# The delta rule's inverse: one evacuation moved from VectorE to ScalarE, with a new table of places

## The chip, the cores and the metric

The kernel runs on one core of one Trainium2 chip. The metric is the device time of one execution in microseconds (us). A core has TensorE (PE, and PEld for its weight loads), VectorE (DVE), ScalarE (ACT), GpSimd (POOL) and SyncE (SP), each with its own queue worked off in order; they wait for one another on semaphores. Matmuls write to PSUM banks, from which VectorE and ScalarE copy.

## The reference

Two blocks run one after the other on 1024 tokens of width 1024. The second is a hybrid mixer with a gated delta rule, followed by a mixture of experts. Only the delta rule matters here. Each of 8 heads (keys and values of width 128) runs it twice, over the sequence and over the reversed sequence. In chunks of tokens, with `t_mat` the inverse of a unit triangular matrix:

```
t_mat = inverse(eye + a_mat)          # a_mat strictly triangular, one per chunk
u = t_mat @ (v * beta);  w = t_mat @ (k_beta * exp(g))
def step(state, inp):                 # one chunk after the other
    v_new = u_c - w_c @ state
    o_c = q_c @ state + qk_c @ v_new
    state = state * dec_c + k_c^T @ v_new
```

The outputs of both directions are added, normalized and gated.

## The kernel before, in words

The stage is `delta_scan`. 1040 tokens are 10 chunks of 104 rows. For each head four programs are written once for every engine:

- `prepare(h)`: transposes of v and k (`v 0..2`, `k 0..2`), gaps of decays (`gap`, L2726, 20 instructions of VectorE), their exp (L2857), products k·k and q·k (`kk`, `qk`, L2537), GpSimd's `nbeta` and `strict` (L2946, L2950), transposes `T 0..4` (L2546, copied by ScalarE at L2863). Transposes and products share one PSUM bank, so each waits until the one before is copied out.
- `invert(h)`: the inverses of both directions from 64 by 64 blocks: five rounds over three units of chunks (4, 3 and 3), so 15 pairs (round, unit). In each, TensorE squares the power (`NT`; ScalarE copies both directions out, L2884, in the last round L2886), and multiplies the sum so far (`P`). In the straight direction VectorE adds the bank to `pc` (L2755). In the crossed one GpSimd first adds one to the power (`nti`, L2979), TensorE's product is then the whole new sum, and VectorE only copies it from its bank to `pc` (L2757). The next P waits for both. After the last: `pt`, `ym`, `w`, which put the blocks together.
- `recur(h)`: ten steps k; TensorE makes KS (L2656), VectorE the right-hand side (L2803), TensorE U (L2670), ScalarE copies U (L2904), TensorE dS (L2676) and the outputs (L2682, L2684), VectorE the new state S (L2813) and sums of outputs (L2784, L2793).
- `finish(h)`: squares and VectorE's `ms` (L2825), GpSimd's power and scaling of the outputs (pow L2997, onorm L2999), transposes `y 0..2` (L2702).

While `recur(h)` runs, `invert(h + 1)`, `finish(h - 1)` and `prepare(h + 2)` are spread over its 30 places, three per step: for TensorE, place 3k stands between KS and U, 3k+1 between U and dS, 3k+2 behind the outputs. For VectorE places 3k and 3k+1 stand between the outputs of step k-1 and S, 3k+2 behind S; for ScalarE 3k stands ahead of U's copy. GpSimd has no step of its own, so places give it only an order. The places of every item on every engine are tables (`a_place`, `b_place`, `take_place`, ...). An item is issued in its place or, where an earlier item of its own program has a later one, right behind that item:

```
def upto(self, place):
    while self.place is not None and self.place <= place:
        self.place = next(self.program, None)
```

Two prologues run ahead of head 0: `prepare(0)`, then `invert(0)` with `prepare(1)`. The last two heads have no `prepare` beside them.

Of the kernel before, what the change touches and what calls it, by code (L numbers as in the profile page):

```python
# [19 lines left out]
ACT = mybir.ActivationFunctionType  # L20
# [3 lines left out]
P = 128  # L24
# [2226 lines left out]
def delta_scan(nc, p2T, qT_d, kT_d, vT_d, gc_d, etot_d, sc_d, dmask_d, strict_d, ident_d, eye_d, gout_d, ydT):  # L2251
# [11 lines left out]
    ROUNDS = 5  # L2263
# [3 lines left out]
    with ExitStack() as ctx:  # L2267
# [76 lines left out]
        a_place = {('v', 0): 2, ('v', 1): 3, ('v', 2): 2, ('k', 0): 4, ('k', 1): 6, ('k', 2): 7, ('kk', 0): 11, ('qk', 0): 12, ('kk', 1): 13, ('qk', 1): 14, ('kk', 2): 15, ('qk', 2): 17, ('T', 0): 18, ('T', 1): 16, ('T', 2): 21, ('T', 3): 24, ('T', 4): 27, ('gap', 0, 0, 0): 1, ('gap', 0, 0, 1): 0, ('gap', 1, 0, 0): 0, ('gap', 1, 0, 1): 0, ('gap', 0, 1, 0): 1, ('gap', 0, 1, 1): 3, ('gap', 1, 1, 0): 1, ('gap', 1, 1, 1): 0}  # L2344
        d_place = {('y', 0): 8, ('y', 1): 9, ('y', 2): 10}
        copy_place = {('exp', 0, 0): 3, ('v', 0): 2, ('exp', 1, 0): 0, ('v', 1): 3, ('exp', 0, 1): 1, ('v', 2): 0, ('exp', 1, 1): 0, ('k', 0): 4, ('k', 1): 6, ('k', 2): 7, ('T', 0): 16, ('T', 1): 18, ('T', 2): 23, ('T', 3): 26, ('T', 4): 27}
        fill_place = {('kk', 0): 11, ('qk', 0): 12, ('kk', 1): 13, ('qk', 1): 14, ('kk', 2): 15, ('qk', 2): 17}
# [1353 lines left out]
```

## Time and profile before

| | |
|---|---|
| time, median of 3 runs | 3744.97 us (3739.28 to 3747.4) |
| the profiled execution | 3753.08 us |
| its span, first to last instruction | 3751.3 us |
| mean granted clock of TensorE | 0.938 of full speed |
| the delta stage from its first inverse on | 589.4 us of the span |

The profile is one execution. In timelines each row is one instruction or a run of like ones (start, duration, engine, line, what it writes and reads, count), and in brackets how long the engine was idle before it and who ended that. Busy times of a stretch are followed by the count of instructions. The count of TensorE's fp32 matmuls is two records each.

### The profile page before, as it was taken

To read this page: it belongs to the slowest core of one execution; us is meant where nothing else is said; L and a number is where in the kernel's file an instruction comes from. 1 tells how busy PE (TensorE), PEld (TensorE's weight loads), DVE (VectorE), ACT (ScalarE), POOL (GpSimd) and SP (SyncE) were. 2 spreads that over 40 slices of the span, in tenths; PEclk is the share of its full clock that TensorE was granted. 3 is DMA by queue.
4 is the path that set the end of the run, shared out by engine and by line. 5 is a ranking of instruction groups with operands and counts; after the bars stand their busy time and mean duration, and the time that the engine had idled before them with its cause. 6 is when DMAs were issued, how large, how long until landed. Compare 5 with 4: busy or idle time off the path is not lost. (4 is left out here: it accounts for less than half of the span.)

```text
span 3751.3 us, 80899 instructions
## 1 busy us (share of the span) xinstructions
PE 3210.4 (86%) x33564; PEld 2675.7 (71%) x33564; DVE 1609.8 (43%) x2654; ACT 944.7 (25%) x1831; POOL 572.1 (15%) x615
## 2 busy tenths in 40 slices
PE   8999999888897979999999568888969995988873
PEld 6878777788775768999999457777859773544431
DVE  3155654334335633111989436665544424111113
ACT  2022311122132212100554234444421110211111
POOL 1000000000001000000323044445410001222222
PEclk9999999999998998999999679999979997999997
DMA  4335455321136333332554321111035238999997
GB/s 126 93 119 195 165 202 190 101 54 45 57 129 229 108 105 96 94 96 93 176 173 145 102 79 46 53 53 42 26 110 167 73 88 341 418 419 417 413 412 296
DMA packets 314850, 595.26 MB, mean 159 GB/s; under 512 B 56993, under 2 KB 221706, under 8 KB 285590
## 3 DMA queue, kind: packets, MB, share of 16 engines
q1 hardware_dynamic: 263348, 455.68, 34.3%
q10 hardware_dynamic: 40329, 118.90, 9.0%
q0 software_dynamic: 10928, 17.08, 1.3%
q8 instruction: 196, 3.21, 0.4%
q14 instruction: 49, 0.40, 0.0%
HBM read 472.36 MB, written 139.97 MB: 163 GB/s over the span
## 5 line engine op out<-in xcount | busy, mean ns | idle before, releaser
L3304 PE MATMUL ex_bank_ps<-ex_w_gate_up_sb,ex_xT_sb 128*64 128x256 f32 x2240 | 282.9, 407 | 87.9 <-DMA ex_w_gate_up_sb<-in_w_up_e 82.1
L3304 PEld LDWEIGHTS ex_bank_ps<-ex_w_gate_up_sb,ex_xT_sb 128*64 128x64 f32 x2240 | 166.0, 141 | 216.9 <-issue 125.7
L260 DVE CAST in_w_hi_sb<-in_w_sb 128x1024 fp32r<-128x1024 f32 x119 | 81.9, 688 | 549.4 <-PE in2n_bank_ps L272 268.1
L272 PE MATMUL in2n_bank_ps<-in_h_hi_sb,in_w_hi_sb 128*128 128x352 f32 (+3 forms) x696 | 224.8, 323 | 2.1 <-DVE in_h_lo_sb L401 2.1
L272 PE MATMUL in2n_bank_ps<-in_h_lo_sb,in_w_hi_sb 128*128 128x352 f32 (+3 forms) x696 | 224.2, 322 | 0.0
L272 PE MATMUL in2n_bank_ps<-in_h_hi_sb,in_w_lo_sb 128*128 128x352 f32 (+3 forms) x696 | 223.7, 321 | 0.0
L1474 PE MATMUL mix_bank_ps<-mix_y_hi_sb,mix_wb_hi_sb 128*128 128x512 f32 (+2 forms) x480 | 170.7, 356 | 56.5 <-DVE mix_y_lo_sb L1705 44.8
L3495 DVE TENSOR_TENSOR ex_hidden_sb<-ex_silu_g_sb,ex_bank_ps 128x128 f32<-128x128 f32 x70 | 20.1, 287 | 443.7 <-ACT ex_silu_g_sb L3356 443.7
L1635 POOL TENSOR_TENSOR mix_y_lo_sb<-mix_raw_sb,mix_y_hi_sb 128x1024 fp32r<-128x1024 f32 (+1 forms) x8 | 20.0, 2498 | 1152.1 <-ACT mix_y_hi_sb L1561 1152.1
L272 PE MATMUL qkv_tile_bank_ps<-in_h_hi_sb,in_w_hi_sb 128*128 128x352 f32 (+1 forms) x576 | 186.0, 323 | 8.8 <-DVE qkv_ones_r_sb L1867 7.9
L272 PE MATMUL qkv_tile_bank_ps<-in_h_lo_sb,in_w_hi_sb 128*128 128x352 f32 (+1 forms) x576 | 185.4, 322 | 0.0
L272 PE MATMUL qkv_tile_bank_ps<-in_h_hi_sb,in_w_lo_sb 128*128 128x352 f32 (+1 forms) x576 | 185.2, 322 | 0.0
L1883 DVE SCALAR_TENSOR_TENSOR qkv_y_sb<-qkv_x_sb,qkv_taps_sb,qkv_y_sb 128x1040 f32<-128x1040 f32 x96 | 182.5, 1901 | 3.4
L1474 PE MATMUL mix_bank_ps<-mix_y_lo_sb,mix_wb_hi_sb 128*128 128x512 f32 (+2 forms) x480 | 169.4, 353 | 0.0
L1474 PE MATMUL mix_bank_ps<-mix_y_hi_sb,mix_wb_lo_sb 128*128 128x512 f32 (+2 forms) x480 | 169.2, 352 | 0.0
L272 PE MATMUL prep_tile_bank_ps<-in_h_hi_sb,in_w_hi_sb 128*128 128x512 f32 x384 | 154.5, 402 | 5.1 <-PEq L159 5.1
L272 PE MATMUL prep_tile_bank_ps<-in_h_lo_sb,in_w_hi_sb 128*128 128x512 f32 x384 | 150.8, 393 | 0.0
L272 PE MATMUL prep_tile_bank_ps<-in_h_hi_sb,in_w_lo_sb 128*128 128x512 f32 x384 | 150.6, 392 | 0.0
L262 DVE TENSOR_TENSOR in_w_lo_sb<-in_w_sb,in_w_hi_sb 128x1024 fp32r<-128x1024 f32 x119 | 145.0, 1219 | 4.1
L1474 PEld LDWEIGHTS mix_bank_ps<-mix_y_hi_sb,mix_wb_hi_sb 128*128 128x128 f32 x480 | 92.0, 192 | 68.0 <-issue 55.6
L272 PEld LDWEIGHTS in2n_bank_ps<-in_h_hi_sb,in_w_hi_sb 128*128 128x128 f32 (+1 forms) x696 | 129.4, 186 | 3.9 <-DVE in_h_lo_sb L401 2.5
L272 PEld LDWEIGHTS in2n_bank_ps<-in_h_hi_sb,in_w_lo_sb 128*128 128x128 f32 (+1 forms) x696 | 129.1, 185 | 1.5
(480 smaller groups left out, 8166.7 us busy)
## 6 DMA issues: line engine op xcount, KB each, us to landing
ex_w_gate_up_sb<-in_w_gate_e SPq DMA_DIRECT2D x70, 1024.0 KB, 19.9
ex_w_gate_up_sb<-in_w_up_e SPq DMA_DIRECT2D x70, 1024.0 KB, 29.8
ex_w_down_sb<-in_w_down_e SPq DMA_DIRECT2D x70, 1024.0 KB, 29.6
in_w_sb<-in_w_in SPq DMA_DIRECT2D x118, 512.0 KB
scr_pT<-in_o_sb ACTq DMA_DIRECT2D x65, 512.0 KB
scr_p2T<-in_o_sb ACTq DMA_DIRECT2D x52, 520.0 KB
qkv_x_sb<-scr_p2T SPq DMA_DIRECT2D x8, 1560.0 KB, 8.1
mix_gate_sb<-scr_pT SPq DMA_DIRECT2D x24, 512.0 KB, 3.5
```

The source lines that it names most:

```text
L260: dve.tensor_copy(self.w_hi[:, s, :, 0:width], w).then_inc(self.w_hi_rdy, 1)
L262: dve.tensor_tensor(self.w_lo[:, s, :, 0:width], w, self.w_hi[:, s, :, 0:width].bitcast(F32), ALU.subtract).then_inc(self.w_split, 1)
L272: last = pe.matmul(self.psum(s, n)[:width, 0:m], w_[:, s, k, 0:width], h_[:, k, a:a + m], start=(k == 0 and z == 0), stop=(k == KT - 1 and ...
L1474: last = pe.matmul(bank[:, 4 * s + c, 0:w], w_[:, s, k, :], y_[:, k0[n] + k, a:a + w], start=(k == 0 and z == 0), stop=(k == kts[n] - 1 an ...
L1635: pool.tensor_tensor(y_lo[:, j, :], raw[:, j % RAW, :], y_hi[:, j, :].bitcast(F32), ALU.subtract).then_inc(y_split_pool, 1)
L1883: ins = v.scalar_tensor_tensor(y[:, q, k % 2, :], x[:, u, q, k:k + N], taps[:, u, q, k:k + 1], y[:, q, (k - 1) % 2, :], ALU.mult, ALU.add)
L3304: last = t.matmul(bank[m * BT:(m + 1) * BT, GU_B + b % 2, 0:2 * P], xT[:, s, k, at:at + BT], wgu[:, ws, :, k, m::M], start=(k == 0), stop= ...
L3495: v.tensor_tensor(h[:, s, :], sg[:, s, :], bank[:, GU_B + s, P:2 * P], ALU.mult).then_inc(h_rdy, 1)
```

## The change

ScalarE copies the crossed sums instead of VectorE: same source, same target, same 15 a head. On ScalarE the copy of P(i-1) stands behind the copies of NT(i). Whoever waited for it on VectorE's semaphore (`vx`) waits on ScalarE's (`ax`). All tables of places are new as well.

```diff
-        ax = Plan(st.sem("act_crossed"), [("NT", *w) for w in powers])
+        ax = Plan(st.sem("act_crossed"), [x for x in pe_order if x[0] in ("NT", "P")])
...
-        vx = Plan(st.sem("dve_crossed"), [("pc", z) for z in range(2)] + [("P", *w) for w in powers])
+        vx = Plan(st.sem("dve_crossed"), [("pc", z) for z in range(2)])
...
                         vb.wait(t, h, "P", *powers[i - 1])
-                        vx.wait(t, h, "P", *powers[i - 1])
+                        ax.wait(t, h, "P", *powers[i - 1])
...
                     vb.step(v.tensor_tensor(pc[:, us(u), :], pc[:, us(u), :], blocks(P_B[0], k), ALU.add), "P", r, u)
-                    px.wait(v, h, "P", r, u)
-                    vx.step(v.tensor_copy(pc[:, us(u, 1), :], blocks(P_B[1], k)), "P", r, u)
...
+                def take_sums(r, u):
+                    yield take_place["P", r, u]
+                    px.wait(a_, h, "P", r, u)
+                    ax.step(a_.activation(pc[:, us(u, 1), :], blocks(P_B[1], len(unit(u))), ACT.Copy), "P", r, u)
+
+                for i, w in enumerate(powers):
+                    yield from take_powers(*w)
+                    if i:
+                        yield from take_sums(*powers[i - 1])
+                yield from take_sums(*powers[-1])
```

What the tables come to on TensorE, by place (P r,u and NT r,u: round and unit):

| place | before | after |
|---|---|---|
| 1 | NT 1,0 | NT 1,0 |
| 2 | NT 1,1, v 0 | NT 1,1, P 1,0 |
| 3 | P 1,0, NT 1,2, v 1, v 2 | v 0 |
| 4 | P 1,1, k 0 | NT 1,2, P 1,1, v 1, v 2, k 0 |
| 6 | NT 2,0, k 1 | NT 2,0, k 1 |
| 7 | k 2 | P 1,2, NT 2,1, k 2 |
| 8 | P 1,2, NT 2,1, P 2,0, y 0 | y 0 |
| 9 | NT 2,2, P 2,1, y 1 | P 2,0, NT 2,2, y 1 |
| 10 | NT 3,0, P 2,2, y 2 | P 2,1, NT 3,0, P 2,2, y 2 |
| 14 | P 3,1, qk 1 | qk 1 |
| 15 | NT 4,0, kk 2 | P 3,1, NT 4,0, kk 2 |
| 16 | P 3,2, NT 4,1, P 4,0 | P 3,2, NT 4,1, P 4,0, qk 2 |
| 17 | qk 2 | NT 4,2 |
| 18 | NT 4,2, T 0, T 1 | T 0, T 1 |
| 19 | P 4,1, NT 5,0 | P 4,1, NT 5,0, T 2 |
| 20 | P 4,2 | - |
| 21 | NT 5,1, P 5,0, T 2 | P 4,2, NT 5,1, P 5,0, T 3 |
| 22 | NT 5,2, P 5,1 | NT 5,2 |
| 23 | P 5,2 | P 5,1 |
| 24 | T 3 | P 5,2, T 4 |
| 27 | ym 1, w 0, T 4 | ym 1 |
| 28 | w 1 | w 0, w 1 |

Places 0, 5, 11 to 13, 25, 26 and 29 are the same in both. On the other engines:

- VectorE: of the 20 gap instructions, 13 stood in place 1 and 7 in place 3; now 8 stand in place 1 and 12 in place 3. The sum of P 1,0 goes from place 4 to 2, that of P 5,2 from 23 to 24, the `w` products from 27 to 28.
- ScalarE: `v 0` to `v 2` stay in place 3, ahead of U's copy of step 1. k 2's copy goes from place 7, behind NT 2,1, to place 6, ahead of U's copy of step 2. T 0's copy stays in place 16, and NT 4,2's goes from ahead of it to behind it.
- GpSimd: the order up to `nti 1,2` is nti 1,0, nti 1,1, pow, onorm, nbeta, strict, nbeta, and a second strict that stood ahead of nti 1,2 and now stands behind nti 2,0. `kd` and `strict` change places with `nti 3,0`.

## Rows read from the trace of the kernel before

**Rows 1.** The page of the kernel before: span, busy time and share by engine
```profile
span 3751.3 us, 80899 instructions
...
PE 3210.4 (86%) x33564; PEld 2675.7 (71%) x33564; DVE 1609.8 (43%) x2654; ACT 944.7 (25%) x1831; POOL 572.1 (15%) x615
```

**Rows 2.** Stretches of the delta stage
```profile
core 0: us, PE busy (x) PEld busy (x) DVE busy (x) ACT busy (x) POOL busy (x), PEclk, DMA share, GB/s
2193.40:2250.80 57.40, 45.36 (x1573) 39.35 (x1576) 26.66 (x74) 24.60 (x55) 32.37 (x35) 0.94 0.11 29
...
2461.60:2531.50 69.90, 62.74 (x1638) 55.98 (x1631) 43.16 (x131) 30.69 (x90) 33.73 (x36) 0.98 0.19 55
...
sum 589.40, PE 505.60 PEld 447.86 DVE 337.13 ACT 240.56 POOL 262.01; mean PE 56.18 PEld 49.76 DVE 37.46 ACT 26.73 POOL 29.11
```

**Rows 3.** TensorE's waits, heads 1 to 5: total us, times, longest
```profile
PE dlt_bank_ps L2557 <- DVE dlt_o_sb L2793: 8.0, 5, 1.7
...
PE dlt_bank_ps L2546 <- ACT dlt_qkT_sb L2863: 4.3, 5, 0.9
PE dlt_bank_ps L2702 <- ACT dlt_ktok_sb L2850: 3.6, 5, 0.8
...
PE dlt_bank_ps L2670 <- DVE dlt_rh_sb L2803: 1.7, 5, 0.3
```

**Rows 4.** VectorE's groups by form, the stage: busy us, mean ns
```profile
L2757 DVE COPY dlt_p_blocks_sb<-dlt_bank_ps 128x192 f32<-128x192 f32 x80 | 28.0, 350 | 0.0
...
L2757 DVE COPY dlt_p_blocks_sb<-dlt_bank_ps 128x256 f32<-128x256 f32 x40 | 16.7, 417 | 0.0
```

**Rows 5.** ScalarE's groups by form, the stage
```profile
L2886 ACT ACTIVATE dlt_powers_sb<-dlt_bank_ps 128x192 f32<-128x192 f32 x32 | 8.7, 325 | 19.9 <-PE dlt_bank_ps L2557 19.9
```

**Rows 6.** Timeline of TensorE: first inverse, then fourth head
```profile
2202.97 0.27 PE L2557 MATMUL dlt_bank_ps<-dlt_p_blocks_sb,dlt_powers_sb 64*64 64x64 f32 x2 [0.93 <-ACT dlt_powers_sb L2884]
...
2471.25 0.43 PE L2525 MATMUL dlt_bank_ps<-dlt_ident_sb,dlt_vT_sb 128*104 128x128 f32 x2 [0.69 <-ACT dlt_vtok_sb L2850]
...
2473.21 0.61 PE L2676 MATMUL dlt_bank_ps<-dlt_U_sb,dlt_k_decayed_sb 104*128 104x128 f32 x4
...
2476.71 0.49 PE L2670 MATMUL dlt_bank_ps<-dlt_rh_sb,dlt_p_sb 104*104 104x128 f32 x3
...
2477.95 0.42 PE L2525 MATMUL dlt_bank_ps<-dlt_ident_sb,dlt_kT_sb 128*104 128x128 f32 x2 [0.64 <-ACT dlt_ktok_sb L2850]
...
2482.85 0.55 PE L2702 MATMUL dlt_bank_ps<-dlt_ident_sb,dlt_o_sb 104*128 104x104 f32 x4 [0.78 <-ACT dlt_ktok_sb L2850]
```

**Rows 7.** Timeline of GpSimd, fourth head
```profile
2469.19 1.97 POOL L2997 TENSOR_TENSOR dlt_rstd_sb<-dlt_ms_sb,dlt_neghalf_sb 104x10 f32<-104x10 f32 x1
2471.24 2.33 POOL L2999 TENSOR_TENSOR dlt_o_sb<-dlt_o_sb,dlt_rstd_sb 104x1280 f32<-104x1280 f32 x1
2473.52 1.06 POOL L2946 TENSOR_TENSOR dlt_nt_sb<-dlt_dd_sb,dlt_sc_sb 104x520 f32<-104x520 f32 x1
...
2478.28 1.28 POOL L2979 TENSOR_TENSOR dlt_nt_and_one_sb<-dlt_powers_sb,dlt_eye_blocks_sb 128x192 f32<-128x192 f32 x2
```

**Rows 8.** Timeline of VectorE, fourth head
```profile
2469.56 1.74 DVE L2726 SCALAR_TENSOR_TENSOR dlt_dd_sb<-dlt_gcr_sb,dlt_sc_sb,dlt_dmask_sb 104x104 f32<-104x104 f32 x7
```

**Rows 9.** Timelines of VectorE and GpSimd before the first inverse
```profile
2161.75 3.88 DVE L2726 SCALAR_TENSOR_TENSOR dlt_dd_sb<-dlt_gcr_sb,dlt_sc_sb,dlt_dmask_sb 104x104 f32<-104x104 f32 x16
...
2162.92 3.63 POOL L2946 TENSOR_TENSOR dlt_nt_sb<-dlt_dd_sb,dlt_sc_sb 104x520 f32<-104x520 f32 x1 [9.29 <-ACT dlt_dd_sb L2857]
```

**Rows 10.** Head 0: VectorE, GpSimd, TensorE, and the stretch behind
```profile
2256.72 5.26 DVE L2726 SCALAR_TENSOR_TENSOR dlt_dd_sb<-dlt_gcr_sb,dlt_sc_sb,dlt_dmask_sb 104x104 f32<-104x104 f32 x7
...
2257.47 1.28 POOL L2950 TENSOR_TENSOR dlt_nt_sb<-dlt_nt_sb,dlt_strict_sb 104x520 f32<-104x520 f32 x1
...
2262.90 0.37 PE L2557 MATMUL dlt_bank_ps<-dlt_p_blocks_sb,dlt_powers_sb 64*64 64x64 f32 x2 [3.62 <-DVE dlt_p_blocks_sb L2757]
...
2262.90:2268.20 5.30, 5.30 (x46) 4.91 (x47) 1.23 (x4) 2.00 (x6) 0.59 (x1) 0.50 0.85 217
```

More of the change, by code:

```diff
@@ L2343, in delta_scan @@
         FILLS = [("kk", 0), ("qk", 0), ("kk", 1), ("qk", 1), ("kk", 2), ("qk", 2)]
[L2344 removed]
+        a_place = {('v', 0): 3, ('v', 1): 4, ('v', 2): 1, ('k', 0): 2, ('k', 1): 6, ('k', 2): 7, ('kk', 0): 11, ('qk', 0): 12, ('kk', 1): 13, ('qk', 1): 14, ('kk', 2): 15, ('qk', 2): 16, ('T', 0): 18, ('T', 1): 14, ('T', 2): 19, ('T', 3): 21, ('T', 4): 24, ('gap', 0, 0, 0): 1, ('gap', 0, 0, 1): 0, ('gap', 1, 0, 0): 0, ('gap', 1, 0, 1): 3, ('gap', 0, 1, 0): 0, ('gap', 0, 1, 1): 0, ('gap', 1, 1, 0): 0, ('gap', 1, 1, 1): 0}
         d_place = {('y', 0): 8, ('y', 1): 9, ('y', 2): 10}
[L2346 to L2347 removed]
+        copy_place = {('exp', 0, 0): 2, ('v', 0): 3, ('exp', 1, 0): 2, ('v', 1): 3, ('exp', 0, 1): 0, ('v', 2): 2, ('exp', 1, 1): 4, ('k', 0): 2, ('k', 1): 5, ('k', 2): 6, ('T', 0): 16, ('T', 1): 18, ('T', 2): 19, ('T', 3): 20, ('T', 4): 29}
+        fill_place = {('kk', 0): 11, ('qk', 0): 13, ('kk', 1): 10, ('qk', 1): 14, ('kk', 2): 15, ('qk', 2): 16}
         pe_order = [("n", f) for f in range(NF)]
@@ L2354, in delta_scan @@
-        pool_place = {('n', 0): 0, ('n', 2): 0, ('NT', 1, 0): 0, ('NT', 1, 1): 1, ('NT', 1, 2): 7, ('NT', 2, 0): 5, ('NT', 2, 1): 9, ('NT', 2, 2): 8, ('NT', 3, 0): 10, ('NT', 3, 1): 20, ('NT', 3, 2): 20, ('NT', 4, 0): 11, ('NT', 4, 1): 19, ('NT', 4, 2): 21, ('NT', 5, 0): 16, ('NT', 5, 1): 22, ('NT', 5, 2): 24, ('p', 0): 21, ('p', 1): 18, 'rstd': 4, ('nbeta', 0, 0): 5, ('strict', 0, 0): 3, ('nbeta', 1, 0): 5, ('strict', 1, 0): 5, ('nbeta', 0, 1): 7, ('strict', 0, 1): 0, ('nbeta', 1, 1): 9, ('strict', 1, 1): 3, ('kd', 0, 0): 14, ('kd', 1, 0): 3, ('kd', 0, 1): 21, ('kd', 1, 1): 16}
@@ new lines, in delta_scan @@
+        pool_place = {('n', 0): 3, ('n', 2): 3, ('NT', 1, 0): 6, ('NT', 1, 1): 0, ('NT', 1, 2): 7, ('NT', 2, 0): 6, ('NT', 2, 1): 8, ('NT', 2, 2): 8, ('NT', 3, 0): 14, ('NT', 3, 1): 17, ('NT', 3, 2): 12, ('NT', 4, 0): 9, ('NT', 4, 1): 16, ('NT', 4, 2): 23, ('NT', 5, 0): 24, ('NT', 5, 1): 14, ('NT', 5, 2): 26, ('p', 0): 16, ('p', 1): 25, 'rstd': 6, ('nbeta', 0, 0): 6, ('strict', 0, 0): 1, ('nbeta', 1, 0): 3, ('strict', 1, 0): 7, ('nbeta', 0, 1): 5, ('strict', 0, 1): 2, ('nbeta', 1, 1): 6, ('strict', 1, 1): 10, ('kd', 0, 0): 10, ('kd', 1, 0): 3, ('kd', 0, 1): 20, ('kd', 1, 1): 16}
@@ L2626, in invert @@
                     vb.wait(t, h, "P", *powers[-1])
-                    vx.wait(t, h, "P", *powers[-1])
+                    ax.wait(t, h, "P", *powers[-1])
                     for j, c in enumerate(hc(g)):
@@ L2876, in invert, with take_powers @@
                     ab.step(a_.activation(to, src, ACT.Copy), "n", f)
-                for r, u in powers:
+                def take_powers(r, u):
                     yield take_place["NT", r, u]
@@ L2983, in invert @@
                     yield pool_place["p", d]
-                    (vx if d else vb).wait(g_, h, "P", ROUNDS, NU - 1)
+                    (ax if d else vb).wait(g_, h, "P", ROUNDS, NU - 1)
                     if h >= 2:
```

6 lines of the change are left out of this document (3 added, 3 removed).

## The prediction

> **What bounds the kernel now.** I read the page first: TensorE is busy for 86% of the span, VectorE for 43%, ScalarE for 25% [rows 1]. Such shares are means over stages, so next I cut out the one stage that the change touches, the delta rule, with the view of stretches: one stretch from the first matmul of the first inverse to the first U copy, then one for each head from U copy to U copy [rows 2]. The reader is to see that the stage is 589.4 of 3751.3 us, so 1% of it is 0.16% of the kernel, and that in a middle head (the fourth, 69.9 us) TensorE works for 62.7 us, VectorE 43.2, ScalarE 30.7 and GpSimd 33.7. Neither the engine that loses work nor the one that gets it is the bound; TensorE is, and its instructions stay the same in number and form. So the change can win or lose only in TensorE's idle 7 us a head, and the whole question is which of its waits goes and which comes. The third view, TensorE's waits over heads 1 to 5, says who holds it [rows 3]: the outputs of the head before (8.0 us in 5), ScalarE's evictions of transposes (4.3 and 3.6 us in 5 each), the right-hand side (1.7 us). A wait on the copy that moves is not among them. Last I walked the fourth head in the timelines of each engine and laid the new order over it.
>
> **The moved copy.** It leaves VectorE 15 times a head: 80 copies of 350 ns and 40 of 417 ns in all, 28.0 + 16.7 = 44.7 us, 5.6 a head [rows 4]. ScalarE gets them at its nearest row, 325 ns for the same 128x192 from the same kind of bank [rows 5]; the 256 form I scale by VectorE's ratio, 417/350, to 387 ns. That is 41.5 us, 5.2 a head. ScalarE's idle 39 us a head covers it; uncovered it would cost 41.5 us, all of it. The gain is in latency: VectorE did sum, then copy, and TensorE's next P waited for both. Side by side this saves one copy, about 0.35 us, wherever that wait was exposed: at P 4,0, P 5,1 and at the right-hand side of step 8, which sat behind a sum and a copy (0.35 us a head [rows 3]). A wait also costs TensorE its overlap of neighbours, some 0.2 us. I take 1.05 us a head for the three; bounds 0.3 and 2.
>
> **The places, step by step in a middle head.** First what they win.
> - y 0 is transposed in place 8 and waits 0.78 us for ScalarE's k 2, which sits behind a power that TensorE has not yet made [rows 6]. In the new order k 2 is out early: 0.78 + 0.2 = about 1.0.
> - T 1 waits 0.87 us for T 0's copy behind two power copies, 4.3 us in five heads [rows 3]. NT 4,2 moves behind T 0 on ScalarE: 0.25.
> - Products of 64 by 64 come in 19 uninterrupted groups instead of 21: 0.4 with the overlap. Smaller such waits that I find, 0.2.
> Won: 1.05 + 1.0 + 0.25 + 0.6 = 2.9 us a head.
>
> What they cost:
> - Step 1. v 1, v 2 and k 0 now all stand behind U and ahead of dS. v 2 still waits for v 1's copy (0.69 [rows 6]); then k 0 waits for v 2's copy, which is behind an exp, and with v 0 alone in place 3 TensorE waits some 0.4 for the right-hand side. dS 1 starts at about 2473.86 instead of 2473.21 [rows 6]: 0.65.
> - Step 2. k 2 comes last in front of dS 2, and ScalarE must copy it before U: 0.76 in place of today's 0.64 [rows 6]: 0.1.
> - P 1,2 moves from place 8 to 7, ahead of dS 2, and needs nti 1,2 from GpSimd. U 2 started 3.5 us after dS 1 [rows 6] and takes 0.5, so P 1,2 is due at 2477.9. GpSimd's queue in front of it is pow, onorm (2.33), two nbeta and one strict [rows 7]; left alone, nti 1,2 would be out at about 2477.6, just in time. But VectorE's gap instructions in place 3 rise from 7 to 12, start at 2469.75 where 7 took 1.74 us [rows 8], so at 0.24 each they end at 2472.7, across onorm's start at 2471.24. The trace shows what follows: where 16 such instructions were running, a GpSimd instruction of 1.06 us took 3.63 and ended 0.9 us after them [rows 9]. So onorm ends at 2472.7 + 2.33 = 2475.0 instead of 2473.56 and nti 1,2 at 2479.0. P 1,2 waits 1.1, 1.25 with the lost overlap. Bounds 0 and 1.5.
> - Step 8. P 5,2 moves to place 24, and VectorE's sum of it stands behind rhs and the outputs of step 7; pt 0 waits for it: 0.6.
> - Step 9. w 0 and T 4 no longer fill the time in front of U 9, and w 1 follows ym 1 closely: 0.25.
> Lost: 0.65 + 0.1 + 1.25 + 0.6 + 0.25 = 2.85 us a head.
>
> Net for five middle heads: 5 x (2.85 - 2.9), nothing; as both sides are sums of small waits I give each head 1.2 us either way.
>
> **A rule weighed against the rows.** Rows 9 show a GpSimd instruction waiting for the end of the whole run of VectorE instructions, 2.6 us longer than its own 1.06; [rows 10] show the reverse, a VectorE run begun while GpSimd worked, 7 instructions in 5.26 us, one behind each GpSimd instruction. The Trainium skill, SBUF — State Buffer, section "SBUF: two separate sides", says that the two engines share a port pair as an exclusive lock, taken by whichever starts first and held for the whole instruction. By that letter onorm would get the pair after one VectorE instruction, and VectorE would be the one held; the sum would be 11 us higher; the second rival below works this case out from the rows.
>
> **The rest of the stage.** In head 0 there is no onorm, and the seven gap instructions are held to 2261.98, with the sum and copy of P 1,0 behind them; TensorE waits 3.62 us for that copy. Behind this wait the granted clock was 0.50, that is 1.2 GHz, for 5.3 us [rows 10]. In the new order that sum is in place 2, ahead of the run. But v 2's copy then waits for an exp that waits for the seventh of the run, so of 3.62 us I count 2.7 as won, and 2 for the clock (5.3 us of work at half speed), less 0.7 for new waits: 4 us. Bounds 1 and 6. In the first inverse P 1,0 waited 0.93 us for a GpSimd instruction held by 20 gap instructions [rows 6]; now 8 stand in front: 0.5 won after a later hold. The last two heads have no prepare: 1 won together, by the sums alone.
>
> Sum: 0 + 4 + 0.5 + 1 = 5.5 us off the profiled execution's 3753.1 us (3751.3 span and 1.8 around it). That execution is 8.1 above the median of the runs shown, 3745.0; I subtract from the median: 3739.5 us. A measurement of this kernel can tell about 0.2%, 7.5 us, from no change.
>
> **The rivals.**
> - The hold on onorm doesn't matter: GpSimd is ahead by a microsecond, or P 1,2 is due later than I have it. For it: only a microsecond separates the two times. Against: the hold is in the trace twice. Then 5 x 1.25 more is won: 3733.
> - The run on VectorE is held instead, as it was in head 0. Seven gap instructions pass during pow; the other five go one behind each of onorm, nbeta, strict, nbeta and nti: to 2477.6. S 1, due at 2474.5, comes 3.4 us late, and nti 1,2 no longer adds its 1.25: 2.15 x 5 = 11 us: 3750.5. Against it: rows 9, where the run came first and kept on.
> - ScalarE becomes the bound and the kernel is slower. Its queue is in order: in places 3 to 8 it now waits for v 2, k 2 and products ahead of U and of the powers, and all 15 copies stand in that queue. 5.2 us a head is the price if all are exposed; it decides from 2 us a head (2 x 7 = 14 against 5.5), which gives 3754. For it: ScalarE already ended 7.9 us of TensorE's waits in five heads [rows 3]. Against: 39 us idle in each.
> - The change does nothing: the relief is hidden behind TensorE, head 0's hold only shifts: 3745.
>
> **How the numbers follow.** Forecast 0.40, no hold 0.22, VectorE held 0.13, ScalarE 0.12, nothing 0.13. The forecast's own range is 3732 to 3747. All together hold eight in ten between 3728 and 3752. Faster by over 0.2% (under 3737.5): two fifths of the forecast, nearly all of the second case, 0.38. Slower (over 3752.5): two thirds of the ScalarE case, a third of the one with VectorE held, something from each other, 0.18. Within: 0.44.
>
> **What would show it.** TensorE's waits on k 2 at the y transposes gone; one of about 1 us on nti 1,2 in heads 1 to 5 in their place; onorm's record about 3.8 us long instead of 2.33; head 0 without its 3.62 us wait and without the slow clock; new waits of 0.6 us at the pt transposes; VectorE's busy time 45 us less, ScalarE's 41 more. I would be wrong above all if VectorE is the one held (gap instructions over 1 us long in heads 1 to 5), if U copies come later behind ScalarE's new work, or if new waits bring the clock down again.

## The result, and the profile after

The kernel became slower. On one chip, the kernel before took 3743.22 us (4 runs) and the changed one 3772.25 us (4 runs, 3769.30 to 3775.13): ratio 1.0077, with a 95% interval of 1.0060 to 1.0095, so +29 us. The two profiled executions differ by less, 3769.3 against 3753.1 us, because the one of before stands at the upper end of its runs and the one of after is the fastest of its own. The traces explain 16 of the 29 us; a second profile of the changed kernel (3778.9 us) is read with them below.

The page of the changed kernel, the lines that answer to [rows 1]:

```profile
span 3767.5 us, 80899 instructions
...
PE 3213.7 (85%) x33564; PEld 2675.7 (71%) x33564; DVE 1593.4 (42%) x2534; ACT 983.5 (26%) x1951; POOL 573.8 (15%) x615
```

VectorE has lost 120 instructions but only 16.4 us of busy time where 44.7 were due. Either the copies weren't worth that, or what is left on VectorE takes longer. The view of stretches of the changed kernel, prologue, then heads 0 to 6 from U copy to U copy:

```profile
core 0: us, PE busy (x) PEld busy (x) DVE busy (x) ACT busy (x) POOL busy (x), PEclk, DMA share, GB/s
2147.80:2253.70 105.90, 68.59 (x1651) 56.28 (x1655) 39.37 (x93) 36.25 (x84) 47.08 (x44) 0.71 0.26 81
2253.70:2321.00 67.30, 60.79 (x1636) 54.07 (x1640) 38.70 (x113) 34.80 (x100) 29.48 (x34) 1.00 0.14 41
2321.00:2395.40 74.40, 65.03 (x1642) 58.45 (x1644) 43.05 (x117) 35.67 (x103) 33.65 (x36) 0.93 0.18 51
2395.40:2468.90 73.50, 61.60 (x1642) 54.72 (x1646) 43.36 (x116) 35.59 (x103) 33.69 (x36) 1.00 0.18 52
2468.90:2543.10 74.20, 64.44 (x1642) 57.30 (x1642) 38.35 (x116) 35.59 (x103) 34.98 (x36) 0.95 0.17 51
2543.10:2616.70 73.60, 63.52 (x1640) 56.42 (x1640) 43.61 (x116) 35.65 (x103) 33.64 (x36) 0.98 0.18 52
2616.70:2690.30 73.60, 62.02 (x1643) 54.96 (x1644) 42.49 (x115) 35.59 (x103) 33.83 (x37) 1.00 0.05 18
2690.30:2749.10 58.80, 52.01 (x1439) 45.64 (x1438) 26.20 (x81) 27.27 (x85) 23.15 (x26) 1.00 0.07 22
```

Before, the same stretches were 101.5 (prologue), 71.8, 69.1, 69.9, 69.9, 69.8, 71.7 and 55.6 us. Head 0 won 4.5 us, as forecast. Heads 1 to 5 lost 5.3, 3.6, 4.3, 3.8 and 1.9 us, the prologue 4.4, head 6 3.2. Cut finer, at the U copies of each step, nearly all of the loss of heads 1 to 5 is in steps 0 to 2: 122.2 us in the five heads before, 141.0 now, while their steps 3 to 9 together went from 228.0 to 228.4. (These steps took over some 60 matmul records with P 2,1, and TensorE had no half clock in them any more, where before it had 3.4 us.) TensorE's waits of heads 1 to 5 (total us, times, longest), to be laid beside [rows 3]:

```profile
PE dlt_bank_ps L2525 <- ACT dlt_vtok_sb L2848: 11.4, 10, 3.3
...
PE dlt_bank_ps L2557 <- issue: 7.2, 6, 1.8
PE dlt_bank_ps L2656 <- DVE dlt_S_sb L2811: 7.0, 3, 2.3
PE dlt_bank_ps L2562 <- issue: 5.1, 4, 2.2
PE dlt_bank_ps L2676 <- ACT dlt_U_sb L2913: 3.7, 5, 0.7
PE dlt_bank_ps L2546 <- ACT dlt_qkT_sb L2861: 3.0, 5, 0.6
```

Of the kernel before, rows of the same view that [rows 3] doesn't show:

```profile
PE dlt_bank_ps L2562 <- issue: 5.9, 6, 1.5
PE dlt_bank_ps L2557 <- issue: 5.2, 4, 1.6
...
PE dlt_bank_ps L2525 <- ACT dlt_vtok_sb L2850: 3.4, 5, 0.7
PE dlt_bank_ps L2525 <- ACT dlt_ktok_sb L2850: 3.2, 5, 0.6
```

The wait at the y transposes is gone and T 1's has shrunk from 4.3 to 3.0. New are the state S (7.0 us in three waits) and U 2 behind k 2's copy (0.75 a head, 3.7 us), and the waits for v rose from 3.4 to 11.4 us. The pauses for which the profile names nobody ("issue") were there before as well: 12.3 us in five heads, 13.2 in this profile, 20.0 in the second one of the changed kernel. Over 7 us of them, in both kernels, are pauses of 1.1 to 1.9 us in step 1 of every head, for which nothing here gives a cause. Others now stand in step 2, and those are followed up below.

**Who is late.** Head 1, in order: VectorE, then ScalarE's exp and its copy of v 2, then TensorE's transpose k 0:

```profile
2329.22 7.71 DVE L2726 SCALAR_TENSOR_TENSOR dlt_dd_sb<-dlt_gcr_sb,dlt_sc_sb,dlt_dmask_sb 104x104 f32<-104x104 f32 x12
```

```profile
2334.98 0.64 ACT L2855 ACTIVATE dlt_dd_sb<-dlt_dd_sb 104x520 f32<-104x520 f32 x1 [2.83 <-DVE dlt_dd_sb L2726]
2335.53 0.37 ACT L2848 ACTIVATE dlt_vtok_sb<-dlt_bank_ps 104x256 f32<-104x256 f32 x1
```

```profile
2335.94 0.88 PE L2525 MATMUL dlt_bank_ps<-dlt_ident_sb,dlt_kT_sb 128*104 128x128 f32 x3 [3.32 <-ACT dlt_vtok_sb L2848]
```

Twelve gap instructions take 7.71 us, where seven took 1.74 [rows 8]. One by one in the trace, four are 0.32 us long; the fifth starts at 2330.17, 0.08 after GpSimd's scaling, and is 2.39 long; the next ones end one behind each GpSimd instruction. That is the rival that I gave 0.13: VectorE is held. In head 2 the run takes 8.28 us and S 1, behind it, is late by the 2.33 that TensorE then waits. Of the five heads VectorE is held in 1, 2, 4 and 5. In head 3 it is the other way round:

```profile
2477.57 3.75 POOL L3008 TENSOR_TENSOR dlt_o_sb<-dlt_o_sb,dlt_rstd_sb 104x1280 f32<-104x1280 f32 x1
```

```profile
2476.21 2.92 DVE L2726 SCALAR_TENSOR_TENSOR dlt_dd_sb<-dlt_gcr_sb,dlt_sc_sb,dlt_dmask_sb 104x104 f32<-104x104 f32 x12
```

Here the scaling is the 3.75 us long that I had foreseen for every head, and no gap instruction is held.

**The clock follows.** Stretches of 6.8 us around head 1's wait of 3.32 us:

```profile
2328.30:2335.10 6.80, 3.40 (x87) 2.45 (x85) 6.74 (x11) 1.95 (x4) 6.64 (x5) 1.00 0.01 4
2335.10:2341.90 6.80, 5.96 (x76) 5.69 (x80) 3.65 (x11) 3.79 (x10) 1.35 (x2) 0.50 0.51 117
2341.90:2348.70 6.80, 6.05 (x178) 5.39 (x174) 1.97 (x7) 3.89 (x11) 5.20 (x5) 1.00 0.36 102
```

TensorE is busy for half of the first stretch, and in the next the granted clock is 0.50, 1.2 GHz: it is busy for as long as in the third, with 76 instead of 178 matmul records. The sums of steps 0 to 2 of heads 1 to 5, before and after:

```profile
sum 122.20, PE 98.42 PEld 86.25 DVE 66.59 ACT 62.06 POOL 76.18; mean PE 19.68 PEld 17.25 DVE 13.32 ACT 12.41 POOL 15.24
sum 141.00, PE 104.18 PEld 89.94 DVE 77.33 ACT 72.44 POOL 80.31; mean PE 20.84 PEld 17.99 DVE 15.47 ACT 14.49 POOL 16.06
```

TensorE's busy time rose by 5.8 us, its idle time from 23.8 to 36.8: of the 18.8 us lost there, 13 are waits. The 5.8 are the clock, and a little less than its share: TensorE has some 60 matmul records fewer in these steps, since P 2,1 moved from place 9 to 10 (some 2.2 us by my estimate, from 36 such records that took 1.25). Stretches at half clock add up to 6.8 us before and 20.5 after.

### The profile page after: what moved, and what is told of

It reads as the page before. It is cut to its first block and busy times, and to the rows that moved or that the text cites. A ratio compares the mean times of both kernels' runs of the same rounds, so it can differ in the third digit from the quotient of the medians.

```text
span 3767.5 us, 80899 instructions
## 1 busy us (share of the span) xinstructions
PE 3213.7 (85%) x33564; PEld 2675.7 (71%) x33564; DVE 1593.4 (42%) x2534; ACT 983.5 (26%) x1951; POOL 573.8 (15%) x615
## 5 line engine op out<-in xcount | busy, mean ns | idle before, releaser
L1474 PEld LDWEIGHTS mix_bank_ps<-mix_y_hi_sb,mix_wb_hi_sb 128*128 128x128 f32 x480 | 91.8, 191 | 69.5 <-issue 55.6
```

Of the source, the lines that this page charges most:

```text
L1474: last = pe.matmul(bank[:, 4 * s + c, 0:w], w_[:, s, k, :], y_[:, k0[n] + k, a:a + w], start=(k == 0 and z == 0), stop=(k == kts[n] - 1 an ...
```

## The experiments

Theory A: the collision of the gap run with GpSimd's scaling, whichever of the two is held. Theory B: the copies in ScalarE's queue. Theory C, added after the first runs: the new order of the early places itself (P 1,2 ahead of dS 2, v and k). The sets of runs were made on different chips, and the kernel before ran beside each set, with medians of 3748.4, 3749.3, 3748.3, 3745.1 and 3746.4 us. The ratios are to the kernel before on the same chip, so times of different sets are compared by them. By its two ratios the changed kernel is 1.0055 to 1.0077. "Steps 0 to 2" is the sum over heads 1 to 5 in the profiled execution.

| kernel | median us | ratio (95%) | steps 0 to 2, us |
|---|---|---|---|
| before | 3743.2 to 3749.3 | 1 | 122.2 |
| after | 3772.25 | 1.0077 (1.0060, 1.0095) | 141.0 |
| after again | 3776.86 | 1.0055 (1.0036, 1.0075) | 145.9 |
| after, gaps 13 and 7 | 3766.38 | 1.0053 (1.0035, 1.0071) | 122.0 |
| the same, sum of P 1,0 late | 3772.51 | 1.0071 (1.0047, 1.0095) | 136.0 |
| before, gaps 8 and 12 | 3753.85 | 1.0019 (1.0008, 1.0031) | 124.8 |
| copies alone | 3759.25 | 1.0032 (1.0021, 1.0044) | 125.9 |
| copies, P 1,0's early | 3750.15 | 1.0008 (0.9997, 1.0019) | 127.7 |
| places alone | 3776.95 | 1.0073 (1.0057, 1.0090) | 138.5 |
| early before, late after | 3753.78 | 1.0011 (0.9993, 1.0030) | 118.9 |
| early after, late before | 3772.35 | 1.0055 (1.0037, 1.0074) | 140.7 |
| after, P 1,2 in place 8 | 3763.26 | 1.0037 (1.0019, 1.0055) | 133.8 |
| after, v and k as before | 3786.15 | 1.0099 (1.0067, 1.0131) | 152.5 |
| after, gaps and P 1,2 | 3748.14 | 1.0012 (1.0001, 1.0022) | 122.1 |
| the same, k 2's copy late | 3745.02 | 0.9998 (0.9986, 1.0010) | 117.8 |
| before, sum of P 1,0 early | 3789.58 | 1.0120 (1.0100, 1.0139) | 159.8 |
| after, decays later | 3767.27 | 1.0055 (1.0040, 1.0069) | 127.3 |
| before, decays later | 3750.61 | 1.0005 (0.9994, 1.0015) | 118.3 |
| best hybrid, decays later | 3748.19 | 1.0006 (0.9997, 1.0015) | 116.8 |

### The gap run and the copies, each by itself

**The changed kernel with the gap places of before.**

```diff
-('gap', 1, 0, 1): 3, ('gap', 0, 1, 0): 0, ('gap', 0, 1, 1): 0
+('gap', 1, 0, 1): 0, ('gap', 0, 1, 0): 1, ('gap', 0, 1, 1): 3
```

> The changed kernel (3772 us) with one thing put back: VectorE's gap instructions in the places of before (13 in place 1, 7 in place 3, in place of 8 and 12). Theory A (collision: in four of five middle heads GpSimd's onorm starts while the longer run of gap instructions is still going and holds it, so S of step 1 is late): the runs end before onorm starts, no gap instruction of heads 1 to 5 takes over 1 us, TensorE's waits for S in step 1 (7.0 us in 3) and the 1.4 to 3.3 us waits at the v transposes go, some 3 us a head, 15 us in all: 3755 to 3759. Rival B (ScalarE's new copies are the loss): no change, 3772. Rival C (the other places: transposes in one clump between U and dS, P 1,2 and NT 2,1 ahead of dS 2): at most 3 us less.

Measured: 3766.4, and a wide spread, 3749 to 3772. Its profile is of its fastest execution, 3749.0: the waits for S gone, those for v down from 11.4 to 5.8 us, steps 0 to 2 as before. The collision isn't gone in it, against the expectation: VectorE is held in heads 2 and 5, by two instructions and by one, of up to 2.39 us. By the ratios this edit alone is worth 1 to 9 us (1.0053 against 1.0055 and 1.0077, with intervals that overlap), which can't be told from nothing, and the profile of the fastest execution doesn't say what is left in the others.

**The kernel before with the gap places of after** (8 and 12, nothing else).

> The kernel before (3743 us) with one thing from the change: 8 gap instructions in place 1 and 12 in place 3. Theory A: gap instructions over 1 us long in heads 1 to 5, S of step 1 late, 10 to 20 us more, 3753 to 3763. Rivals B and C: nothing, within 3 us of before.

Measured: 1.0019, +5.5 us. In all five heads GpSimd is the one held, and VectorE runs through. Head 2:

```profile
2402.68 3.44 POOL L2999 TENSOR_TENSOR dlt_o_sb<-dlt_o_sb,dlt_rstd_sb 104x1280 f32<-104x1280 f32 x1
```

```profile
2401.00 2.93 DVE L2726 SCALAR_TENSOR_TENSOR dlt_dd_sb<-dlt_gcr_sb,dlt_sc_sb,dlt_dmask_sb 104x104 f32<-104x104 f32 x12
```

With the run held off nothing, it is only long: the sum and copy of P 1,0 stand behind it, and TensorE waits 1.2 us a head for that copy.

**The copies alone**: the code of the changed kernel with all places of before, each crossed sum copied by ScalarE in the place where VectorE took it.

```diff
-    px.wait(v, h, "P", r, u)
-    vx.step(v.tensor_copy(pc[:, us(u, 1), :], blocks(P_B[1], k)), "P", r, u)
+    yield take_place["P", r, u]     # the place that sum_place had
+    px.wait(a_, h, "P", r, u)
+    ax.step(a_.activation(pc[:, us(u, 1), :], blocks(P_B[1], len(unit(u))), ACT.Copy), "P", r, u)
```

> The copy of the crossed sums on ScalarE, behind the next power's copies as in the change, all other tables as in the kernel before (ScalarE takes each copy in the place that VectorE had for it). Theory A and rival C: the copy costs nothing, 3738 to 3746. Rival B: the 15 copies a head delay U's copies and the powers, 15 to 29 us more than before, 3758 to 3772.

Measured: 1.0032, +11 us. So the copy isn't a small gain by itself. TensorE's waits of heads 1 to 5 have a new first row:

```profile
PE dlt_bank_ps L2557 <- ACT dlt_p_blocks_sb L2890: 8.2, 10, 1.3
```

Five of the ten are P 1,1, 1.3 us each: in place 4, P 1,0's copy stands in ScalarE's queue behind the three copies of v and the exps of place 3.

**The same with that one copy in place 3**, ahead of the copies of v.

```diff
-'P', 1, 0): 4
+'P', 1, 0): 3
```

> The copies on ScalarE with all the places of before, and only the crossed sum of P 1,0 taken one place earlier on ScalarE, ahead of the copies of v. If what made the copy alone cost 11 us is that this one copy stands in ScalarE's queue behind the v copies (TensorE waited about 1.25 us a head for it), that wait goes and the time comes to 3740 to 3750; if the cost is spread over all 15 copies (ScalarE as a bound), it stays at 3755 to 3762.

Measured: 1.0008, back at the kernel before. (Its profile is of one of its longest executions, 3758.4 us; in head 1 the run of seven collided with the scaling there, took 5.74 us, and steps 0 to 2 of that head took 30.4 us instead of 24.) Theory B holds for one copy of 15, through its place in the queue, and that place the changed kernel had already mended. It is no part of the loss.

**The places alone**: the new tables, VectorE still copies.

> All new places as in the changed kernel, but VectorE still copies the crossed sums, behind its own sum of each pair. Theory A (the collision of VectorE's run of 12 gap instructions with GpSimd's scaling of the outputs is the loss, with whatever else the new places do): the loss stays, 3760 to 3780, gap instructions over 1 us long in heads 1 to 5, TensorE's waits for the new state S of 1 us and more. Theory B (the copy in ScalarE's queue is the loss): 3743 to 3752, near the kernel before.

Measured: 1.0073, all of the loss. But its profile turns half of theory A down: here GpSimd is held in four of the five heads (scaling 3.74 to 3.94 us) and VectorE in one, and the time is as long as with VectorE held in four. The waits for S are 1.0 us, and the pauses without a name are 10.9 and 6.5 instead of 7.2 and 5.1:

```profile
PE dlt_bank_ps L2557 <- issue: 10.9, 9, 2.4
...
PE dlt_bank_ps L2562 <- issue: 6.5, 5, 2.0
```

**The changed kernel once more.**

> The changed kernel once more, nothing altered: 3765 to 3776. A second profile of it says whether it is always the same engine that is held in the first steps. If VectorE is held in most heads again, theory A's reading of the first profile stands; if GpSimd is held in most and the time is as long, the length doesn't hang on which of the two waits.

Measured: 3776.9. The engine held changes from execution to execution: now VectorE in heads 2 and 5, GpSimd in 1, 3 and 4, at the same places in the program. The waits for S fell to 2.3 us and the pauses rose to 9.8 and 8.5. What one side spares the other takes.

Steps 3 to 9 differ as well: 232.1 us with the places alone, where the changed kernel has 228.4 and 227.2 and the kernel before 228.0. At the new places the copy moved to ScalarE wins 3.7 to 4.9 us in these steps of the profiles; what it wins, the new places had lost.

**The changed kernel with 13 and 7, and the sum of P 1,0 behind the run.**

> The changed kernel with 13 gap instructions in place 1 and 7 in place 3, as before, and VectorE's sum of P 1,0 back in place 4, so that the run of 7 starts earlier against GpSimd's power and can end before the scaling of the outputs begins. If the collision explains the spread of the kernel with 13 and 7 (3749 to 3772), no gap instruction is over 1 us long and the times lie within 6 us of each other at 3745 to 3756. If its level has another cause (places of the first steps, copy), it stays near 3766.

Measured: 3772.5, 3763 to 3789: a miss, and by my own edit. P 1,1 in place 4 needs that sum, which now stood behind the run: TensorE waited 0.9 us a head for it, and 4.9 in head 2, where the run was held. It says nothing on the spread.

### Which places

**Exchange of the early and the late half**, with P 2,2 as the border and ScalarE's copies in all. With the two pure kernels this is a table of two by two: early and late as before 1.0008, only late as after 1.0011, only early as after 1.0055, both 1.0055 and 1.0077.

> The changed kernel (ScalarE copies), with the places of everything up to P 2,2 (gaps, v, k, first two rounds, GpSimd's scaling) as in the kernel before and everything later as in the changed one. Theory A/C, that the loss of some 25 us is made in steps 0 to 2 by the new early places: it is gone, 3742 to 3752, steps 0 to 2 of heads 1 to 5 at 24 to 25 us each and the rest of a head 45.2. Rival, that the late places cost it (the rest of head 6 grew from 38.1 to 40.9 us, and TensorE's clock there): 3760 or more.

> The mirror of it: everything up to P 2,2 as in the changed kernel, everything later as before. Theory A/C: nearly the whole loss, 3768 to 3778, steps 0 to 2 of heads 1 to 5 at 27 to 29 us in the mean. Rival (late places): 3745 to 3755.

Measured: 3753.8 and 3772.4. The early places make the loss; the late ones cost nothing that shows, at most some 4 us by the medians, less than the intervals can part.

**P 1,2 and NT 2,1 back in place 8**, in an else unchanged kernel after.

```diff
-('P', 1, 2): 7, ('NT', 2, 1): 4
+('P', 1, 2): 8, ('NT', 2, 1): 8
```

> The changed kernel with P 1,2 and NT 2,1 alone back in TensorE's place 8, behind the outputs of step 2 instead of between U 2 and dS 2 (two profiles show 4.8 and 10.2 us in five heads of waits inside that group, ahead of dS 2, and slow clock behind them). If these waits in the chain are the main loss: 3752 to 3762 and the waits inside step 2 gone. If the hold of VectorE or the v and k transposes are: within 4 us of the changed kernel, about 3770 to 3777.

Measured: 1.0037, by the ratios 7 to 15 us less than the changed kernel. The pauses inside step 2 are gone in all five heads, though the collision was there in each: the scaling was held in two of them, VectorE in three.

**v and k on TensorE and ScalarE as before.**

> The changed kernel with the transposes of v and k on TensorE and their copies and exps on ScalarE alone in the places of before: v 0 in 2, v 1 and v 2 in 3, k 0 in 4, k 2's copy behind U 2 again. TensorE's waits for copies of v came to 11.4 us in the five heads and those for U 2 to 3.7, against 10.2 for v and k before; the wait at y 0 of 0.8 a head comes back. If this cluster is the main loss: 3752 to 3762. If the place of P 1,2 or the hold is: 3768 to 3777.

Measured: 1.0099, slower still. The new places of v and k weren't the loss, they softened it. The three v copies stand ahead of U's copy in ScalarE's queue in both tables; what comes back ahead of it here is the fourth exp, which needs the last gap instructions (in the changed kernel it stands behind U's copy, in place 4). A held run on VectorE (all five heads here) therefore delays that exp and then U 1, for which TensorE waits 12.0 us in five, beside 17.4 for the copies of v.

**Both undone: gaps 13 and 7, P 1,2 in place 8.**

> The changed kernel with both undone at once: 13 and 7 gap instructions, and P 1,2 with NT 2,1 in place 8. If the two are the cause and add up (10 and 12): 3750 to 3756. If they are one wait counted twice, it stays near either alone: 3761 to 3766. Steps 0 to 2 of heads 1 to 5 at 23.5 to 25 us in the first case.

Measured: 3748.1, ratio 1.0012. Undone together, the two edits take back all but 0.12%: 16 to 24 us by the ratios, where each alone took back 1 to 9 and 7 to 15. So the two places together are the cause of the loss; whether their shares add up, the ratios can't say. The sum row of steps 0 to 2, to be held against 122.2 before and 141.0 after:

```profile
sum 122.10, PE 97.39 PEld 83.41 DVE 65.67 ACT 72.33 POOL 80.05; mean PE 19.48 PEld 16.68 DVE 13.13 ACT 14.47 POOL 16.01
```

The collision itself is not gone. VectorE is still held in heads 2, 4 and 5, in head 2 for the whole run of seven:

```profile
2397.23 5.75 DVE L2726 SCALAR_TENSOR_TENSOR dlt_dd_sb<-dlt_gcr_sb,dlt_sc_sb,dlt_dmask_sb 104x104 f32<-104x104 f32 x7
```

Steps 0 to 2 of that head took 25.1 us, against 24.9 before. A hold of this length costs nothing here: the fourth exp, which waits for it, stands behind U's copy in ScalarE's queue. With the places of before it stands ahead of it, and there a hold of 5.74 us went with 6 us more (head 1 of the copies with P 1,0's early). So what costs is the delay that is passed on down the queues, not the hold by itself.

**And k 2's copy behind U 2 again.**

```diff
-('k', 2): 6
+('k', 2): 7
```

> The same and k 2's copy behind U 2 again. TensorE's wait for U 2 of 0.75 us a head goes and the one at y 0 of 0.78 comes back: my step that counted moving it as 1.0 us a head won makes this one 5 us slower than the kernel with both undone; if the wait for U 2 is its equal price, the two agree within 3 us.

Measured: 3745.0 in the same set, 3 us less and not 5 more. The expected return of y 0's wait failed: neither that wait (0.8) nor U 2's (0.75) is in its trace, since k 2's copy now stands behind U 2's but still ahead of NT 2,1's in ScalarE's queue. The gain at y 0 was real, but the changed kernel paid 0.75 us a head at U 2 for it (3.7 in five), and this hybrid has it without. VectorE is held here too, in heads 2 to 5, by one instruction of 2.39 us:

```profile
2460.21 3.81 DVE L2726 SCALAR_TENSOR_TENSOR dlt_dd_sb<-dlt_gcr_sb,dlt_sc_sb,dlt_dmask_sb 104x104 f32<-104x104 f32 x7
```

This is the best hybrid, and it equals the kernel before (0.9986 to 1.0010), no more.

### The collision by itself

**The kernel before with VectorE's sum and copy of P 1,0 ahead of its seven gap instructions.**

```diff
-sum_place = {('P', 1, 0): 4,
+sum_place = {('P', 1, 0): 3,
```

> The kernel before with VectorE's sum and copy of P 1,0 one place earlier, ahead of its run of 7 gap instructions. If head 0's wait of 3.62 us and the slow clock behind it can be had without the rest, and the later run of 7 doesn't meet GpSimd's scaling: 3741 to 3747 against 3748. If VectorE waits for P 1,0 ahead of the run and S or the scaling is late in heads 1 to 5: 3750 or more.

Measured: +44 us, the largest effect of all, by one number in a table. VectorE waits for P 1,0, so the run starts 2 us behind the scaling's start and into GpSimd's row of nbeta and strict. Head 3, VectorE and then GpSimd:

```profile
2490.57 5.74 DVE L2726 SCALAR_TENSOR_TENSOR dlt_dd_sb<-dlt_gcr_sb,dlt_sc_sb,dlt_dmask_sb 104x104 f32<-104x104 f32 x7
```

```profile
2488.60 2.33 POOL L2999 TENSOR_TENSOR dlt_o_sb<-dlt_o_sb,dlt_rstd_sb 104x1280 f32<-104x1280 f32 x1
2490.88 1.08 POOL L2946 TENSOR_TENSOR dlt_nt_sb<-dlt_dd_sb,dlt_sc_sb 104x520 f32<-104x520 f32 x1
```

Seven instructions take 5.74 us instead of 1.74, in all five heads, and GpSimd is never held. TensorE's waits:

```profile
PE dlt_bank_ps L2525 <- ACT dlt_vtok_sb L2850: 18.9, 10, 3.1
PE dlt_bank_ps L2676 <- ACT dlt_U_sb L2904: 16.6, 5, 3.6
```

Of the 37.6 us that steps 0 to 2 are longer, 27 are waits and 10.6 the clock. VectorE's lateness is multiplied on its way: a run 4 us longer, begun 2 us later, is 7.5 us a head on TensorE, since exp, v 2 and U 1 stand in line behind it (v 2's copy behind the third exp, U 1's behind the fourth). So the kernel before is fast because its seven gap instructions run during GpSimd's power: the last starts 0.24 to 0.26 us ahead of the scaling, which leaves a margin of one instruction. The forecast had not seen that margin.

### The pauses in step 2

The pause of 3.23 us in head 4 of the second profile, on TensorE:

```profile
2563.27 0.25 PE L2557 MATMUL dlt_bank_ps<-dlt_powers_sb 64*64 64x64 f32 x2
2566.76 0.37 PE L2562 MATMUL dlt_bank_ps<-dlt_powers_sb 64*64 64x64 f32 x2 [3.23 <-issue]
```

It is in the middle of NT 2,1, whose inputs are all there; P 1,2 ahead of it had waited only 0.71 us, for `nti 1,2`. The DMA view from 2555 to 2567 us of that profile (busy tenths of the 16 engines in 40 slices):

```profile
DMA  0000000757979687467698999997743200000000
...
q8 instruction: 1, 0.02, 0.6%
...
dlt_gcr_sb<-scr_gc SPq DMA_DIRECT2D x2, 422.5 KB
```

SyncE loads the next decays once the last gap instruction is done, here at 2556.3, and the DMA engines are busy from 2557.1 to about 2564.9. The only packet of the queue named "instruction" (16 KB) in the window starts at 2564.44, takes 1.07 us, and TensorE goes on 1.25 us after it. The packet before it was at 2551.66. The pause has the look of a fetch of instructions that came late behind this load; the queue names no engine, so that the packet is TensorE's is inferred. There is a control in every profile: head 5 has no such load, and in the two profiles of the changed kernel its third fetch stands 13.7 and 13.4 us behind U 0, in heads 1 to 4 at 16.7 to 21.8; no pause over 1 us follows in it. (Not every late fetch shows: in the first profile only heads 2 and 3 have a pause, 1.81 and 2.18 us, in the second all four.) In the kernel before pauses of 1.24, 1.49 and 1.14 us are there too, but in place 8, behind the outputs. In place 7 the same group stands between U 2 and dS 2, and the pause is in the chain from state to state.

**The load moved**, in three kernels: SyncE waits in addition until VectorE has taken kk 0, in place 11.

```diff
                 if h:
                     va.wait(sp, h - 1, "gap", *pairs[-1], 1)
+                if h >= 3:
+                    va.wait(sp, h - 1, "kk", 0, 1)
```

> The changed kernel; SyncE's load of the next decays waits in addition until VectorE has taken kk 0 in place 11. If the instruction fetch behind this load is what P 1,2's place costs: the pauses of 1.5 to 3.2 us inside step 2 of heads 1 to 4 go, the third fetch of a head comes at 13 to 15 us instead of 17 to 22, and the time is 3755 to 3765. If the load has nothing to do with it: 3770 to 3777, same pauses.

> The kernel before with the same later load. Its pauses behind the outputs of step 2 (1.24, 1.49, 1.14 us in three of heads 1 to 4) go if they are the fetch: 3738 to 3745 against 3745 to 3749. If the pause only moves with the load to step 4: no change.

> The best hybrid (13 and 7, P 1,2 in place 8, k 2's copy late) with the same later load: 3738 to 3744 if the fetch costs it 1 us a head and its clock stays up; 3743 to 3747 if not.

Measured: in the changed kernel the pauses over 1 us in step 2 are gone in all heads, the waits inside that step without a name are 2.1 us in five (all at `nti 1,2`) instead of 4.8 and 10.2, and the third fetch of the kernel before comes at 12.6 to 12.9 us instead of 15.6 to 17.0 in heads 1 to 4. In the changed kernel it came at 14.4 and 14.1 us in heads 1 and 4, but at 17.8 and 18.2 in heads 2 and 3, outside the 13 to 15 expected, and with no pause there. So the load does make the pause, which goes when the load goes; that it does so by a late fetch is inferred, and how late a fetch is after U 0 doesn't by itself tell a pause. By the ratio 1.0055 the gain is 0 to 8 us, and the other two win nothing: pauses of 0.8 to 2.4 us now stand in steps 5 and 6, where the load went, and steps 3 to 9 rose from 228.4 to 235.5 us in the changed kernel, from 228.0 to 234.9 in the kernel before. Moving the load moves the pause.

## Why the prediction was wrong

It said 3739.5 us (3728 to 3752); the time was 3772.3, +29 where I had -5.5.

The step that failed is the sum for the middle heads, 2.85 us lost against 2.9 won, so nothing in sum. In steps 0 to 2 it had 2.0 lost, 1.25 of it for the collision (through P 1,2), less 1.0 won at y 0; measured were 3.8 and 4.7 us lost a head in the two profiles, and steps 3 to 9, where the other gains were to come, took as long as before. Two things stood in place of the forecast: a collision whose delay is passed on through ScalarE's queue and the clock, whichever engine is held, and a pause of TensorE behind the load of the decays, in the chain between the states since P 1,2 stands in place 7. Undoing both gave back all but 0.12%.

- **Which engine the collision holds.** Forecast: GpSimd, in every head, "as the trace shows" in [rows 9]; VectorE got 0.13. Measured: VectorE in 4 of 5 heads of one execution, in 2 of 5 of another, in 1 of 5 with the copies left on VectorE. My rows 9 and 10 showed one case each, and I took one for the rule. The rule of the Trainium skill, SBUF — State Buffer, section "SBUF: two separate sides" (whoever starts first has the port pair for the whole instruction, the other blocks) agrees with VectorE's rows here: a gap instruction that starts 0.07 to 0.20 us after the scaling is 2.39 long and ends about 0.1 behind it. By its letter, head 3's scaling would have got the pair after one gap instruction; it waited for the rest of the run, 1.56 us. And by its letter the power should have held gap instructions too, as it had started first; it held none.
- **The price of the collision.** Step 2 of the forecast priced it at 1.25 us a head, the rival with VectorE held at 2.15. Both were too low by the same two omissions. What stands behind the late instruction in ScalarE's queue was left out (v 2's copy behind exp: 3.32 us in head 1), and so was the clock in the middle heads, though [rows 10] had shown a wait of 3.62 us with a half clock behind it. Where the queue passes nothing on, the price is near nothing, as the two hybrids with the gaps at 13 and 7 show.
- **P 1,2 in place 7.** The wait for `nti 1,2` was 0.7 us where it occurred, near the 1.1. It occurred only in heads in which GpSimd was held. The step failed by what it didn't have: the pause of 1.7 to 3.2 us behind the load of the decays. By the ratios this place is worth 7 to 15 us, where the forecast had 1.25 a head, 6 us, for another reason. [rows 3] left such pauses out as they had no releaser that the change touches, although the two groups of them, 5.9 and 5.2 us, were the largest entry of that view together.
- **y 0's wait, 1.0 won.** The wait went, but 0.75 us at U 2 took its place. In step 2 I had set this off against the 0.64 of k 2 in the queue of TensorE, and counted 0.1. Undoing half of the move, at U 2 alone, made the kernel 3 us faster. (The 7.9 us for which TensorE already waited for ScalarE in [rows 3] were two rows of four: with v and k at the transposes, 3.4 and 3.2 us, it was 14.5 us in five heads.)
- **The moved copy, 1.05 won.** Steps 3 to 9, where P 4,0, P 5,1 and step 8 are, took 228.4 us in five heads instead of 228.0. T 1 won its 0.25 (4.3 to 3.0 us in five) and the pt transposes wait 0.4 instead of the 0.6 forecast, so against the kernel before they won nothing that shows. The copy itself did win there: with the new places and VectorE still copying, steps 3 to 9 took 232.1 us, so 3.7 to 4.9 us in five heads, near the 5.25 forecast. The new places had cost as much. The copies themselves cost what I said: 38.8 us more on ScalarE for 41.5. VectorE's 45 us less came to 16.4, since held instructions count as busy.
- **Head 0** was right: 4.5 us won for 4, the wait of 3.62 gone and the clock at 1.00. **The prologue** was wrong in sign: 4.4 us longer in the first profile and 1.8 in the second, with 61.0 and 51.2 us at half clock against 51.1. In the profiles with the new early places it took 102 to 106 us, in those with the old ones unedited 100 to 103. **Head 6** lost 3.2 us where I had a gain; each half of the tables is behind about half of it.

ScalarE as the bound (0.12) gave the nearest time, 3754, and was not what happened. The forecast looked at each place by itself in one head of one execution; the loss is of links between three engines, SyncE's loads and the clock. Left open are 29 us by the medians against 16 and 26 in the spans of the two profiles, how the loss divides between the collision and the pause, and the pauses in step 1. Which engine is held has an order that I had not looked for. Take the heads in which the gap run was still going when the scaling was due, in all profiles but that of the kernel before with the sum early. Where the run had started at most 0.52 us after the start of GpSimd's power, GpSimd was held (12 of 12 heads); from 0.77 us on it was VectorE (26 of 28); at 0.68 to 0.69 us each was held in 8 of 16. No run was made to test this, and what decides between executions at 0.68 us stays open.

## What to carry to other kernels

A long run of VectorE instructions beside GpSimd work is one block in a schedule: place it so that it ends before the GpSimd instruction starts, and price the miss from both sides, since either engine may be the one held. The hold alone may cost nothing, as it did with seven gap instructions held for 5.75 us in front of an exp that stood behind U's copy; it costs what the queues pass on. Follow a delay through the queues of the engines behind it before giving it a price: a run held for 4 us on VectorE became 7.5 us on TensorE here, and a wait of 3 us brought 7 us at half clock after it. A pause that the profile puts to nobody still has a cause: compare it with the instruction packets and with the loads that run at that time, and don't put a group of many small matmuls into the chain just behind such a load.

## What the runs showed of the hardware

- A run of back-to-back VectorE instructions that had started first kept a GpSimd instruction from working until the last of them had ended, not only one of them: 3.44 to 3.94 us instead of 2.33, in 21 heads of the profiles read here.
- The other way round, VectorE got one instruction in behind each GpSimd instruction (2.39, then 1.11, 1.43 us), as long as GpSimd had work; in heads 2, 4 and 5 one of 2.46 us waited out two of them. In all five heads of the kernel before with the sum early it was 5.74 us for seven instead of 1.74.
- GpSimd's power of 104x10 elements, 1.97 us, held no gap instruction in any head.
- A DMA queue named "instruction" brings packets of 16 KB, about one in 4 to 5 us in stretches of 64 by 64 products. Under a load that kept the DMA engines busy at 40 to 90% for 8 us, one came 12.8 us after the one before, and TensorE stood for 3.23 us until 1.25 us after it started. With the load moved, the pause was gone from step 2 in all heads.
- The same collision cost 44 us in one schedule (the kernel before with the sum early) and nothing that shows in another (gaps at 13 and 7, P 1,2 in place 8), by what stood behind it in ScalarE's queue.
